# A two-layer hybrid trunk on one core: another order of the setup and the end, later group sums, and attention scores from rounded parts

## The reference

```python
h = modulate(rms_norm(x, ffn1_norm[l]), sh1, sc1)
x = x + 0.5 * g1 * swiglu(h, ffn1_w_in[l], ffn1_w_out[l])
h = modulate(rms_norm(x, mix_norm[l]), sh2, sc2)
q, k, v, u, gates = split(h @ w_mix_in[l])
o = diff_attention(q, k, v, lam, rel_bias)      # 8 heads, two maps each
y_attn = rms_norm(o, subln_gain[l]) * (1 - lam_init) @ w_attn_branch[l]
y_conv = conformer_conv(u, ...)                 # GLU, depthwise width 31, LayerNorm, silu
x = x + g2 * ((sigmoid(ga) * y_attn + sigmoid(gb) * y_conv) @ w_mix_out[l])
h = modulate(rms_norm(x, ffn2_norm[l]), sh3, sc3)
x = x + 0.5 * g3 * swiglu(h, ffn2_w_in[l], ffn2_w_out[l])
```

## Time and profile before

| | us |
|---|---|
| median of 3 runs (lowest, highest) | 2574.42 (2573.01, 2575.19) |
| profiled execution, its own time | 2577.65 |
| its span | 2576.0 |
| TensorE busy | 2514.0 |
| VectorE busy | 1675.6 |
| ScalarE busy | 966.4 |
| POOL busy | 115.8 |
| granted TensorE clock, mean | 0.989 of full speed |

### The profile page before, as it was taken

How to read it: one execution, slowest core, us unless ns; L and a number is a source line. 1 busy time by engine, 2 the same in 40 slices (tenths; PEclk the granted TensorE clock), 3 DMA queues, 4 the chain that set the end, 5 groups by cost and what they waited for, 6 DMA issues and landing times.

```text
span 2576.0 us, 34560 instructions
## 1 busy us (share of the span) xinstructions
PE 2514.0 (98%) x11378; PEld 2033.8 (79%) x11378; DVE 1675.6 (65%) x2493; ACT 966.4 (38%) x1625; POOL 115.8 (4%) x186
## 2 busy tenths in 40 slices
PE   5899999999999999999999999999999999999997
PEld 4788887777778888888878888877777888788886
DVE  6555578798988675543365557778989865643333
ACT  3222323545444343232243232255455443423222
POOL 2100010000000000000000001100000000000000
PEclk7899999999999999999999999999999999999998
DMA  6655475232232334543335555722232233333332
GB/s 215 182 161 157 148 237 160 81 87 82 84 89 83 101 120 131 161 125 93 103 89 158 161 163 188 228 78 84 83 87 80 86 98 98 90 94 95 96 96 94
DMA packets 470157, 311.97 MB, mean 121 GB/s; under 512 B 10723, under 2 KB 447205, under 8 KB 470084
## 3 DMA queue, kind: packets, MB, share of 16 engines
q1 hardware_dynamic: 445078, 227.63, 30.4%
q0 software_dynamic: 22144, 78.40, 9.4%
q10 hardware_dynamic: 2878, 5.20, 0.7%
HBM read 306.46 MB, written 5.05 MB: 121 GB/s over the span
## 4 chain that ended last, share of the span: by engine, by line
PE 84%; DVE 8%; issue 3%; ACT 3%; DMA 1%; ACTq 0%; POOL 0%; DVEq 0%; POOLq 0%; SPq 0%
PE bank L1307 26%; PE bank L1309 25%; PE bank L1308 25%; PE bank L1498 2%; DVE ada_acc L853 1%; PE bank L1477 1%; ACT w_hi L418 1%; DVE rstd L732 1%; DVE w_lo L715 1%; PE bank L1469 1%; DVE scaled L743 1%; DVE h_lo L752 1%; PE bank L1329 1%; DMA bias_rows<-bias_row 1%; PE bank L1334 0%
## 5 line engine op out<-in xcount | busy, mean ns | idle before, releaser
L715 DVE TENSOR_TENSOR w_lo<-w_raw,w_hi 128x1024 fp32r<-128x1024 f32 (+1 forms) x432 | 520.0, 1204 | 562.9 <-ACT w_hi L418 562.4
L1307 PE MATMUL bank<-h_hi,w_hi 128*128 128x512 f32 x2112 | 840.0, 398 | 9.1 <-DVE scaled L993 9.0
L1309 PE MATMUL bank<-h_hi,w_lo 128*128 128x512 f32 x2112 | 824.1, 390 | 0.0
L1308 PE MATMUL bank<-h_lo,w_hi 128*128 128x512 f32 x2112 | 823.8, 390 | 0.0
L418 ACT ACTIVATE w_hi<-w_raw 128x1024 fp32r<-128x1024 f32 (+1 forms) x432 | 449.5, 1041 | 864.1 <-PE bank L1309 807.0
L1307 PEld LDWEIGHTS bank<-h_hi,w_hi 128*128 128x128 f32 x2112 | 397.3, 188 | 100.2 <-issue 18.8
L1309 PEld LDWEIGHTS bank<-h_hi,w_lo 128*128 128x128 f32 x2112 | 397.0, 188 | 84.3
L1308 PEld LDWEIGHTS bank<-h_lo,w_hi 128*128 128x128 f32 x2112 | 397.7, 188 | 77.9 <-issue 0.5
L1097 DVE SCALAR_TENSOR_TENSOR conv_part<-glu,conv_taps,conv_part 128x512 f32<-128x512 f32 x464 | 318.9, 746 | 0.0
L1307 PE MATMUL bank<-s_hi,w_hi 128*128 128x512 f32 x704 | 274.6, 390 | 0.0
L1309 PE MATMUL bank<-s_hi,w_lo 128*128 128x512 f32 x704 | 274.0, 389 | 0.0
(11 more groups left out here) (199 smaller groups left out, 2535.1 us busy)
## 6 DMA issues: line engine op xcount, KB each, us to landing
w_raw<-in_ffn_w_in SPq DMA_DIRECT2D x176, 512.0 KB, 3.8
ada_raw<-in_ada_w POOLq DMA_DIRECT2D x128, 512.0 KB, 4.9
w_raw<-in_w_mix_in SPq DMA_DIRECT2D x112, 512.0 KB, 3.7
w_raw<-in_ffn_w_out SPq DMA_DIRECT2D x64, 512.0 KB, 3.8
w_raw<-in_ffn_w_out SPq DMA_DIRECT2D x32, 384.0 KB, 3.4
w_raw<-in_w_mix_out SPq DMA_DIRECT2D x18, 512.0 KB, 3.7
ada_first<-in_ada_w POOLq DMA_DIRECT2D x16, 512.0 KB, 10.8
w_raw<-in_w_attn_branch SPq DMA_DIRECT2D x16, 512.0 KB, 3.8
```

The source lines that it names most:

```text
L715: dve.tensor_tensor(wlo[slot][:, 0:n, :], raw[slot][:, 0:n, :], whi[slot][:, 0:n, :].bitcast(F32), ALU.subtract).then_inc(w_lo[slot], 1)
L1307: pe.matmul(acc, wh, hi[:, k0 + k, :], start=first and k == 0, stop=False)
L1308: pe.matmul(acc, wh, lo[:, k0 + k, :], start=False, stop=False)
L1309: mm = pe.matmul(acc, wl, hi[:, k0 + k, :], start=False, stop=last and k == n - 1)
```

## The change

- **Setup.** POOL issues the shift and lambda loads right after the scale loads, without waiting for `row_rstd` or for the first slabs; it stores the bias rows before it waits for `lam_dots`. TensorE transposes x first and makes the bias rows then; VectorE does the bias table after the fourth multiply-add; `w_lo_part(0, 0)` moves behind the scale columns. ScalarE copies x before the bias rows, splits both first slabs before it scales the identity, and copies RSTD after `plain_hi`. Its wait for the bias stores moves behind the loop over the tiles of the first FFN.
- **Later group sums.** In ffn1_out `mod_sum_parts` moves from k = 2 to k = 5 of the last slab.
- **Scores.** Query and key are split into rounded and rest parts; a score set is three products of each map (QHI KHI, QHI KLO, QLO KHI), maps in turn. VectorE makes the rest parts and frees the banks. The convolution taps are cut into other groups.
- **The end.** During the last ffn2_out, X times its gain is transposed and copied to `YO`, tile by tile, and the squares' sums go to four columns (one for each block of 128 tokens), the last tile's from `SQ` itself. Root and reciprocal are of [128, 4]; rows are scaled in `YO` on VectorE (blocks 0, 1) and ScalarE (blocks 2, 3), and stored in four pieces of whole rows. The two unused slabs are gone.

```diff
-    QT = at("q_t", [P, TOK], F32, ph)
-    KTT = at("k_t", [P, TOK], F32, ph + 2 * KB)
+    QHI = at("q_hi", [P, TOK], F32R, ph)
+    KHI = at("k_hi", [P, TOK], F32R, ph + 2 * KB)
+    QLO = at("q_lo", [P, TOK], F32R, raw_at)
+    KLO = at("k_lo", [P, TOK], F32R, raw_at + 2 * KB)
...
-        for s in range(2):
-            slab(DEPTH * PAIRS, s, cols(w_mo, 0, 8, 0))
...
+        for n in range(QB):
+            t = n // 2 + 2 * (n % 2)
+            sp.wait_ge(sem("y_last"), QB)
+            sp.wait_ge(sem(("y_scaled_dve", "y_scaled_act")[n % 2]), n // 2 + 1)
+            sp.dma_start(out[0, t * P:(t + 1) * P, :], YO[:, t, :]).then_inc(sem("y_out"), 16)
+        sp.wait_ge(sem("y_out"), 16 * QB)
...
-        pool.wait_ge(sem("minus_half"), 1)
-        pool.wait_ge(sem("row_var"), 1)
-        pool.tensor_tensor(row_rstd[:, :], row_var[:, :], minus_half[:, :].to_broadcast([P, QB]), ALU.pow)\
-            .then_inc(sem("row_rstd"), 1)
-        for s in range(2):
-            pool.wait_ge(w_raw[s], 16)
         for k in range(KT):
             pool.dma_start(ADA0[:, k, 0:D], w_ada[:, k, 0:D]).then_inc(sem(f"ada0_shift{k}"), 16)
...
+        pool.wait_ge(sem("minus_half"), 1)
+        pool.wait_ge(sem("row_var"), 1)
+        pool.tensor_tensor(row_rstd[:, :], row_var[:, :], minus_half[:, :].to_broadcast([P, QB]), ALU.pow)\
+            .then_inc(sem("row_rstd"), 1)
...
-        pool.wait_ge(sem("lam_dots"), 2 * DEPTH)
         pool.wait_ge(sem("br_copied"), 2)
...
+        pool.wait_ge(sem("lam_dots"), 2 * DEPTH)
         pool.wait_ge(sem("br_out"), 16 * HEADS)
         pool.wait_ge(sem("mod_summed"), 1)
...
+        def out_gain(j):
+            if j >= 2:
+                act.wait_ge(sem("yt_ready"), j - 1)
+            act.activation(T[j % 2][:, :], X[:, j, :], ACT.Copy, scale=PT2[:, j:j + 1]).then_inc(sem("y_gained"), 1)
+        def out_copy(j):
+            act.wait_ge(sem("yt_ready"), j + 1)
+            act.activation(YO[:, :, j * P:(j + 1) * P], TP[j % 2][:, :].rearrange("p (t c) -> p t c", c=P), ACT.Copy)\
+                .then_inc(sem("y_copied"), 1)
...
-        act.wait_ge(sem("br_ready"), 1)
-        act.activation(BR[:, 0:TOK], TP[1][:, :], ACT.Copy).then_inc(sem("br_copied"), 1)
-        act.activation(BR[:, TOK:TOK + P], TP[0][:, 0:P], ACT.Copy).then_inc(sem("br_copied"), 1)
...
+        act.wait_ge(sem("br_ready"), 1)
+        act.activation(BR[:, 0:TOK], TP[1][:, :], ACT.Copy).then_inc(sem("br_copied"), 1)
+        act.activation(BR[:, TOK:TOK + P], TP[0][:, 0:P], ACT.Copy).then_inc(sem("br_copied"), 1)
...
+        for s in range(2):
+            w_hi_part(0, s)
         act.wait_ge(sem("ssum_clear"), 1)
...
-        for s in range(2):
-            w_hi_part(0, s)
-        act.wait_ge(sem("aux_ready"), 1)
-        act.activation(RSTD[:, :], AUX[:, :], ACT.Copy, scale=float(D)).then_inc(sem("aux_read"), 1)
         act.wait_ge(sem("cw_ready"), DEPTH)
         for j in range(KT):
             plain_hi(0, j)
+        act.wait_ge(sem("aux_ready"), 1)
+        act.activation(RSTD[:, :], AUX[:, :], ACT.Copy, scale=float(D)).then_inc(sem("aux_read"), 1)
...
+                with act.Fori(2, FT) as i:
+                    ffn_tile(i)
                 if l == 0 and w == 0:
                     act.wait_ge(sem("br_out"), 16 * HEADS)
                     act.dma_start(BD[HEADS, :].rearrange("(p x) -> p x", p=P), BD[0, :].rearrange("(p x) -> p x", p=P))\
                         .then_inc(sem("br_again"), 16)
                     load_bias_tile(0)
-                with act.Fori(2, FT) as i:
-                    ffn_tile(i)
-                if l == 0 and w == 0:
                     act.wait_ge(sem("lam_dots"), 2 * DEPTH)
-                    act.wait_ge(sem("br_again"), 16)
                     act.activation(lam_exp[:, :], lam_dot[:, :], ACT.Exp).then_inc(sem("lam_exps"), 1)
...
+                            if last:
+                                out_gain(i * 2 + m // 3)
+                        if not (last and i == KT // 2 - 1 and m >= 4):
+                            w_hi_part(l * PAIRS + PAIR0[n_out] + i * 3 + m // 2 + 1, m % 2,
+                                      OUTG[(m + 2) % 3] if m < 4 else 8)
+                        if m % 3 == 2 and not last:
                             plain_hi(l * 3 + 1 + 2 * w, i * 2 + m // 3)
+                        if last and m == 5:
+                            out_copy(i * 2)
+                        if last and m == 2 and i:
+                            out_copy(i * 2 - 1)
+                        if last and (i, m) == (KT // 2 - 1, 3):
+                            act.activation(root_warm[:, :], eps[:, :], ACT.Sqrt)
...
-                        act.wait_ge(sem("shift_read"), 2 * (l * 3 + 2))
-                        act.activation(QT[:, :], F[1][:, :], ACT.Identity, bias=wshift[:, 0:1], scale=-HD ** -0.5)\
-                            .then_inc(sem("first_qk"), 1)
-                        act.activation(KTT[:, :], SQ[:, :], ACT.Identity, bias=wshift[:, 1:2]).then_inc(sem("first_qk"), 1)
+                        act.wait_ge(sem("first_qk"), 2 * l + 2)
+                        act.activation(QHI[:, :], F[1][:, :], ACT.Copy).then_inc(sem("qk_hi"), 1)
+                        act.activation(KHI[:, :], SQ[:, :], ACT.Copy).then_inc(sem("qk_hi"), 1)
                     else:
                         weights(1, hh - 1)
                         w_hi_part(p + 1, 0)
-                        act.activation(QT[:, :], G[0][:, :], ACT.Copy, scale=-HD ** -0.5).then_inc(acc_read[0], 1)
+                        act.activation(QHI[:, :], G[0][:, :], ACT.Copy, scale=-HD ** -0.5).then_inc(sem("qk_hi"), 1)
...
-                        act.activation(KTT[:, :], G[1][:, :], ACT.Copy).then_inc(acc_read[1], 1)
+                        act.activation(KHI[:, :], G[1][:, :], ACT.Copy).then_inc(sem("qk_hi"), 1)
...
+        act.wait_ge(sem("y_means"), 1)
+        act.activation(yroot[:, :], AUX[:, 0:QB], ACT.Sqrt, bias=eps[:, 0:1]).then_inc(sem("y_root"), 1)
+        act.wait_ge(sem("y_rstd"), 1)
+        for t in (2, 3):
+            act.activation(YO[:, t, 0:D - P], YO[:, t, 0:D - P], ACT.Copy, scale=yrstd[:, t:t + 1]).then_inc(sem("y_scaled_act"), 1)
...
-            if k == KT - 1:
-                w_lo_part(0, 0)
             first_step(1, "scale", k)
+            if k == 3:
+                bias_table()
...
+        w_lo_part(0, 0)
...
+                    def query_lo():
+                        dve.wait_ge(sem("qk_hi"), 2 * hh + 1)
+                        dve.scalar_tensor_tensor(out=QLO[:, :], in0=G[0][:, :], scalar=-HD ** -0.5, in1=QHI[:, :].bitcast(F32),
+                                                 op0=ALU.mult, op1=ALU.subtract).then_inc(acc_read[0], 1)
+                    def key_lo():
+                        dve.wait_ge(sem("qk_hi"), 2 * hh + 2)
+                        dve.tensor_tensor(KLO[:, :], G[1][:, :], KHI[:, :].bitcast(F32), ALU.subtract).then_inc(acc_read[1], 1)
+                    if first:
+                        n = l * 3 + 1
+                        dve.wait_ge(sem("shift_read"), 2 * n + 2)
+                        dve.tensor_scalar(F[1][:, :], F[1][:, :], -HD ** -0.5, wshift[:, 0:1], ALU.mult, ALU.add).then_inc(sem("first_qk"), 1)
+                        dve.tensor_scalar(SQ[:, :], SQ[:, :], wshift[:, 1:2], None, ALU.add).then_inc(sem("first_qk"), 1)
+                        for m, (lo, full, hi) in enumerate(((QLO, F[1], QHI), (KLO, SQ, KHI))):
+                            dve.wait_ge(sem("first_qk"), 2 * l + m + 1)
+                            dve.wait_ge(sem("qk_hi"), 2 * hh + m + 1)
+                            dve.tensor_tensor(lo[:, :], full[:, :], hi[:, :].bitcast(F32), ALU.subtract).then_inc(sem("first_lo"), 1)
+                    else:
+                        conv(0, 4)
+                        query_lo()
+                        conv(4, 7)
                         w_lo_part(p + 1, 0)
-                    conv(8, 16)
-                    if not first:
+                        conv(7, 14)
                         w_lo_part(p + 1, 1)
-                    conv(16, 21)
+                        key_lo()
+                        conv(14, 19)
                     w_lo_part(p + 2, 0)
-                    conv(21, 23)
+                    conv(19, 21)
                     dve.wait_ge(sem("bt_in"), (hh + 1) * 16)
                     scores(3)
                     if not first:
                         head_lo(hh - 1, tile(AOLO2, h - 1), tile(AOHI2, h - 1))
-                    conv(23, 26)
+                    conv(21, 24)
                     scores(2)
                     row_scales(3)
                     w_lo_part(p + 2, 1)
                     combine(3)
-                    conv(26, 28)
+                    conv(24, 27)
                     scores(1)
                     row_scales(2)
                     w_lo_part(p + 3, 0)
                     combine(2)
-                    conv(28, 29)
+                    conv(27, 29)
...
+        j = KT - 1
```

(43 more changed lines are left out.)

104 lines of the change are left out of this document (50 added, 54 removed).

## The result

| | median | lowest, highest | runs | ratio to before, 95% interval |
|---|---|---|---|---|
| before | 2574.44 us | 2573.01, 2575.19 | 4 | |
| after | 2558.01 us | 2557.01, 2559.7 | 4 | 0.9936 [0.9921, 0.9951] |

A forecast was written before the change was run, and what follows sets the result against it. TensorE, busy 98% of the span, was taken as the bound. Terms -10.8 + 2.7 - 4.0 - 4.4 + 0.5 + 4.0 - 9.6 = -21.6 gave 2556.1 us in the profile, 2552.9 against the median; range 2545 to 2562.

The forecast's parts named there:

- Rival 5: Hole at 87.6 us: returns as a DMA wait, bias stores and weights colliding; half of 10.8 us, 2558; chance 0.07.
- Hole, -10.8: TensorE's stop at 87.6 us: earlier bias stores and a later ScalarE wait remove it and its slow-clock matmuls, -10.8 us.
- Setup, +2.7: Before the first main matmul: slab 1 lands late beside POOL's early loads, moving the chain behind it by +2.7 us.
- The upper bound (+4): Setup: the worst case forecast, +4 us if slab 1 lands at 36.5.
- Rival 2: Setup: no penalty, slab 1 lands as before, -3.0 in place of +2.7, 2547; chance 0.15.
- Group sums, -4.0: ffn1_out's last slab: at k = 5 VectorE's sums are done, saving 8 x 0.51, -4.0 us.
- Scores, -4.4: Score sets in the heads: three rounded passes per map, the maps' halves overlapping; -0.28 per head, 16 heads, -4.4 us.
- +0.5 for head 0: Charge of +0.5 us for both key_lo's late bank release and each layer's head 0 query and key steps.
- Rival 3: Head loop: VectorE becomes the bound, 0.4 to all of its 1.4 us on the path, 14 heads, 2558 to 2572; chance 0.10.
- rival 4: Score sets: weight loads not hidden on half rows, +0.3 per head, +4.7 us in all, 2562; chance 0.05.
- Last ffn2_out, +4.0: Inside the last FFN: 28 transposes and 8 fp32 records of token sums on TensorE's path, +4.0 us.
- Tail, -9.6: After the last main matmul: first store at 2559.0, not 2567.04, four whole-row stores; -9.6 us, bounds -7.5 and -11.

The follow-up runs named there:

- the second run: The kernel before with only ScalarE's wait for the bias stores moved behind the loop over tiles 2 to 21, POOL's stores still late: 2576.82 us, ratio 1.0006.
- the seven runs with 12.3 us: Seven of the eight follow-up runs on the changed kernel that keep the new tail code; last main matmul to the end took 12.30 or 12.31 us.

## Why the prediction was right, and where it wasn't

**The total.** The median is 5.0 us above the forecast. 3.6 of these are the sum's (-21.6 against -18.0); the rest is that the profiled execution lay 3.2 us over its median before the change and only 1.7 after it. The setup's error alone is 3.1 us. Rival 5 had the measured time, 2558, by chance: what it describes didn't happen.

**Hole, -10.8: right in size, half right in reason.** The stretch gave -10.8. The prediction said of the two moves that "both matter"; POOL's order alone gives all of it. ScalarE's is worth 2.8 us only where the stores stay late, and nothing more behind POOL's. The other sentence there, that the stores also share the DMA engines with the weight loads, is what the second run showed. Rival 5 didn't come: issued at 58.64 the stores hold nobody up.

**Setup, +2.7: the mis-sized term, +5.8.** The mechanism was right: slab 1 late beside POOL's loads, and the chain behind it. The failed step is "so w_hi(0, 1) at 35.3": it came at 38.56, and `plain_hi(0)` at 40.69 in place of 37.5. Its 4.2 MB behind the scale loads are the eight shift loads alone. The eight lambda loads, issued right behind them, were left out: 0.26 MB, 0.7 us at 400 GB/s by their bytes, but 2.1 us by the run that held them. About 1.1 us is left: even without them slab 1 was split at 36.42, so the shift loads held it longer than their bytes over 400 GB/s, and no run divides this further. The upper bound (+4) was also too near. Rival 2, the setup without penalty, is what the kernel with POOL's loads held shows: -4.1 at the first main matmul. The Trainium skill (DMA: Bandwidth & Descriptors, Queues, rings and completion order) has the engine go round its queues packet by packet; read as equal bytes that gave slab 1 at 29, and 38.56 excludes that reading.

**Group sums, -4.0:** -4.06 in the trace, 4.3 by the undoing.

**Scores, -4.4 with +0.5 for head 0:** -3.3. Sets of 0.90, 0.73, 0.55, 0.48 were predicted as 0.88, 0.71, 0.56, 0.53; per head 2.66 against 2.96 measured before, and 40.56 against 40.80. The overlap of the halves is shown by the run with both maps on one half. In head 0 the four VectorE and two ScalarE steps end 0.37 us late in each layer (0.69 in place of 0.32 ahead of the first set): the +0.5, at 0.7. The sets alone give 0.30 us a head and a head is only 0.24 shorter; the rest went into its main matmuls (34.17 us, before 34.09), why isn't known. Rival 3 stayed away, but by 0.05 to 0.22 us in most heads, not by 0.3: the prediction took the late waits of VectorE as cover, and the run with `key_lo` twice shows that they don't cover this place.

The Trainium skill (TensorE: Matmul & The Clock Gate, Part 3) says that a weight load overlaps matmuls in flight only where the row group differs, and by that each pass would bear its load (rival 4). The trace disagrees twice: the second and third passes of a set follow each other after 0.12 and 0.11 us at 256 and 128 keys, shorter than one weight load (0.19, the mean of the profile's weight load groups); and on one half alone, where the rule forbids all overlap, six passes took 1.58 us at 512 keys, which is 0.2 and six times 0.23, with no room for loads either.

Rival 4's price was too low for what it says: two loads of 0.19 us more in each of four sets are 1.5 us a head, 24 us in all, not the 9 between -4.4 and +4.7.

**Last ffn2_out, +4.0:** +4.4. **Tail, -9.6:** -10.25; the first store left 6.2 us after the last main matmul, predicted 6.4, and the four stores needed 6.9 instead of 7.4. In the seven runs with 12.3 us the tail gave -11.1, just past the bound of -11: the prediction had counted on the lower clock in the last sums, and there it came later.

## What to carry to other kernels

A load that is issued early costs what stands behind the load it delays, in program order: before moving loads forward, look which engine's next instruction waits for the slower queue, and move the independent chain ahead of it. Count small loads by the time that their pieces take, not by their bytes. And when two moves together close a hole, try each alone: here one makes the whole gain by itself, and the other is worth 2.8 us only without it. Read such a run by stages too: its total said "nothing", and two stages said -2.8 and +2.5.
